# FoX stage of a streaming encoder: turning 128x128 tiles one at a time inside the dense chunk instead of in sets behind it

## The reference

```python
def block(args):
    i, qi, ci = args
    sc = jnp.einsum('bqhd,bkhd->bhqk', qi, k) * SCALE
    sc = sc + ci[..., :, None] - cum[:, :, None, :]
    sc = jnp.where(kpos[None, :] <= qpos[:, None], sc, -jnp.inf)
    p = jax.nn.softmax(sc, axis=-1)
    return jnp.einsum('bhqk,bkhd->bqhd', p, v)
```

## Time and profile before

| | |
|---|---|
| median of 3 runs | 1555.41 us (1554.9 to 1557.6) |
| the profiled execution, span from first to last instruction | 1553.1 us |
| its own time | not among the three runs; its span is the figure for it |
| PE busy (matmul records) | 1495.8 us, 96%, 9803 matmuls |
| DVE, ACT, POOL busy | 1020.4 us (66%), 607.5 us (39%), 611.0 us (39%) |
| chain that ended last | PE 80%, DVE 9% |

### The profile page before, as it was taken

How to read it: one execution, slowest core, us unless ns; L and a number is a source line. 1 busy time by engine, 2 the same in 40 slices (tenths; PEclk the granted TensorE clock), 3 DMA queues, 4 the chain that set the end, 5 groups by cost and what they waited for, 6 DMA issues and landing times.

```text
span 1553.1 us, 25753 instructions
## 1 busy us (share of the span) xinstructions
PE 1495.8 (96%) x9803; PEld 1397.5 (90%) x9803; DVE 1020.4 (66%) x2016; ACT 607.5 (39%) x1256; POOL 611.0 (39%) x407
## 2 busy tenths in 40 slices
PE   6999999999999999999999999999999999999997
PEld 5889999999997998899788999999999999778885
DVE  6866667767674357867445896555555555578986
ACT  5143534435342235666223333333333332444463
POOL 6522232222222322225231568888888781000104
PEclk9999999999999999999999999999999999999999
DMA  6232222222132721129431122222222228723568
GB/s 199 63 94 74 74 87 65 73 70 70 30 97 75 233 95 38 56 82 291 156 108 58 45 67 86 83 83 83 70 83 68 71 83 278 240 97 116 170 195 156
DMA packets 156475, 165.41 MB, mean 107 GB/s; under 512 B 14005, under 2 KB 121913, under 8 KB 156353
## 3 DMA queue, kind: packets, MB, share of 16 engines
q1 hardware_dynamic: 119689, 109.34, 22.6%
q10 hardware_dynamic: 34840, 51.14, 10.0%
q0 software_dynamic: 1824, 3.28, 1.5%
HBM read 125.56 MB, written 39.85 MB: 107 GB/s over the span
## 4 chain that ended last, share of the span: by engine, by line
PE 80%; DVE 9%; DMA 3%; POOL 3%; ACT 2%; issue 2%; ACTq 1%; SPq 0%; DVEq 0%; POOLq 0%
PE bank L1138 16%; PE bank L1140 16%; PE bank L1139 16%; PE bank L1144 6%; PE bank L1146 6%; PE bank L1145 6%; PE bank L1170 4%; PE bank L1279 2%; PE bank L1250 1%; PE bank L1249 1%; DVE p L2649 1%; DVE rowsn L2408 1%; DVE p L2625 1%; POOL ring_l L1080 1%; PE bank L1629 1%
## 5 line engine op out<-in xcount | busy, mean ns | idle before, releaser
L1138 PE MATMUL bank<-ht_h,ring_h 128*128 128x352 f32 x816 | 268.9, 330 | 1.8 <-POOL ring_l L961 1.1
L1140 PE MATMUL bank<-ht_h,ring_l 128*128 128x352 f32 x816 | 263.2, 323 | 0.0
L1139 PE MATMUL bank<-ht_l,ring_h 128*128 128x352 f32 x816 | 262.6, 322 | 0.0
L960 POOL TENSOR_TENSOR ring_h<-raw,att 128x1024 fp32r<-128x1024 f32 x42 | 86.5, 2059 | 405.6 <-PE bank L1140 396.8
L1138 PE MATMUL bank<-m_h,ring_h 128*128 128x264 f32 x648 | 184.2, 284 | 1.2 <-DVE m_l L2895 1.2
L1139 PE MATMUL bank<-m_l,ring_h 128*128 128x264 f32 x648 | 184.2, 284 | 0.0
L1140 PE MATMUL bank<-m_h,ring_l 128*128 128x264 f32 x648 | 183.9, 284 | 0.0
L1138 PEld LDWEIGHTS bank<-ht_h,ring_h 128*128 128x128 f32 x816 | 153.8, 189 | 5.3 <-issue 2.0
L1139 PEld LDWEIGHTS bank<-ht_l,ring_h 128*128 128x128 f32 x816 | 154.6, 189 | 0.7
L1140 PEld LDWEIGHTS bank<-ht_h,ring_l 128*128 128x128 f32 x816 | 153.9, 189 | 0.0
L1138 PE MATMUL bank<-tb_h,ring_h 128*128 128x264 f32 x456 | 129.9, 285 | 0.2 <-DVE u2s L2909 0.2
(11 more groups left out here) (383 smaller groups left out, 3844.9 us busy)
## 6 DMA issues: line engine op xcount, KB each, us to landing
raw<-in_w_up SPq DMA_DIRECT2D x44, 512.0 KB, 3.9
raw<-in_w_in SPq DMA_DIRECT2D x34, 512.0 KB, 3.9
rb<-in_w_down SPq DMA_DIRECT2D x66, 256.0 KB, 2.9
d_y<-conv SPq DMA_DIRECT2D x22, 529.0 KB, 3.3
d_gate<-gst ACTq DMA_DIRECT2D x48, 176.0 KB, 1.9
a<-d_y SPq DMA_DIRECT2D x33, 256.0 KB, 6.1
ra<-d_y SPq DMA_DIRECT2D x33, 256.0 KB, 3.1
gm<-d_gate ACTq DMA_DIRECT2D x8, 528.0 KB, 4.4
```

What stands on the lines that cost most here:

```text
L960: order.link(nc.gpsimd.tensor_tensor(high, src, zero.to_broadcast(list(src.shape)), ALU.add))
L1138: nc.tensor.matmul(out, wh, xh, start=start, stop=False, skip_group_check=onto)
L1139: nc.tensor.matmul(out, wh, xl, start=False, stop=False, skip_group_check=onto)
L1140: return nc.tensor.matmul(out, wl, xh, start=False, stop=stop, skip_group_check=onto)
```

## The change

`dense_chunk` gets a function `turn`, called behind each of its 24 matmuls with the number m of the matmul (0 to 23). In FoX steps with a chunk this function issues the turns one by one, never two behind the same matmul: with n probability tiles, turn j goes behind matmul 24-n+j, so the last one stands behind the chunk's last matmul. In row steps, row tiles 0 to 7 go behind matmuls 0 to 7 and the ninth behind matmul 22-n. The grouping into sets, the banks, the number of turns, and what ACT, DVE and POOL do stay as they are; the waits for a free bank stand before the first turn of each set, that for p_ready before the first probability turn, and that for the keys or values before the first row turn. Without a chunk the turns are issued as before. The row tiles of step (0,0) stay behind the chunk.

```diff
--- before.py
+++ after.py
@@ -1145,7 +1145,11 @@
                 nc.tensor.matmul(out, th, wl, start=False, stop=False, skip_group_check=onto)
                 return nc.tensor.matmul(out, tl, wh, start=False, stop=stop, skip_group_check=onto)
 
-            def dense_chunk(n, c, k_tiles=KT, xh=ht_h, xl=ht_l, col=0, q=None):
+            def no_turn(m):
+
+                return
+
+            def dense_chunk(n, c, k_tiles=KT, xh=ht_h, xl=ht_l, col=0, q=None, turn=no_turn):
 
                 q = position(n, c) if q is None else q
                 pe.wait_ge(slab_split, n + 1)
@@ -1153,11 +1157,16 @@
                 s = n % NSPL
                 wh = flat(ring_h[:, s]).rearrange("p (k c) -> p k c", k=k_tiles)
                 wl = flat(ring_l[:, s]).rearrange("p (k c) -> p k c", k=k_tiles)
+                out, sl = bank[q % 3][:, 0:CH], slice(CH * c, CH * c + CH)
                 for k in range(k_tiles):
-                    mm = three(bank[q % 3][:, 0:CH], wh[:, k, col:col + P], wl[:, k, col:col + P],
-                               xh[:, k, CH * c:CH * c + CH], xl[:, k, CH * c:CH * c + CH],
-                               k == 0, k == k_tiles - 1)
-                mm.then_inc(chunk_full, 1)
+                    nc.tensor.matmul(out, wh[:, k, col:col + P], xh[:, k, sl], start=k == 0, stop=False)
+                    turn(3 * k)
+                    nc.tensor.matmul(out, wh[:, k, col:col + P], xl[:, k, sl], start=False, stop=False)
+                    turn(3 * k + 1)
+                    mm = nc.tensor.matmul(out, wl[:, k, col:col + P], xh[:, k, sl], start=False, stop=k == k_tiles - 1)
+                    if k == k_tiles - 1:
+                        mm.then_inc(chunk_full, 1)
+                    turn(3 * k + 2)
 
             ti = [0]
 
@@ -1254,12 +1263,31 @@
                                               start=False, stop=True)
                     mm.then_inc(s_full, 1)
 
-            def prob_transposes(g):
-                h, b, r = UNITS[g % NU]
-                pe.wait_ge(p_ready, g + 1)
-                assert ti[0] == at_unit[g]
-                for o, w in halves(b, r):
-                    transposes(lambda bk: [(bk[:, i:i + P], ssb[:, g % 2, o + i:o + i + P]) for i in range(0, w, P)])
+            def prob_turn(g, j):
+
+                tiles = width(*UNITS[g % NU][1:]) // P
+                i = at_unit[g] + j // 4
+                if j == 0:
+                    assert ti[0] == i
+                    pe.wait_ge(p_ready, g + 1)
+                if j % 4 == 0:
+                    wait(pe, t_free, i - 1)
+                mm = nc.tensor.transpose(tbank(i)[:, P * (j % 4):P * (j % 4) + P], ssb[:, g % 2, P * j:P * j + P], ident)
+                if j % 4 == 3 or j == tiles - 1:
+                    mm.then_inc(t_full, 1)
+                    ti[0] += 1
+
+            def row_turn(src, i0, j):
+
+                i = i0 + j // 4
+                if j % 4 == 0:
+                    assert ti[0] == i
+                    wait(pe, t_free, i - 1)
+                r = rows(j)
+                mm = nc.tensor.transpose(tbank(i)[0:r, P * (j % 4):P * (j % 4) + P], src[:, P * j:P * j + r], ident)
+                if j in (3, 7, NT):
+                    mm.then_inc(t_full, 1)
+                    ti[0] += 1
 
             def values(v):
                 p, j = divmod(v, V_PAIR)
@@ -1305,22 +1333,33 @@
                         if s % HEAD_U == 0:
                             pe.wait_ge(kq_ready, 2 * p + s // HEAD_U + 1)
                         scores(p, s)
-                    for n, c in fillers(p, s) if g else ():
-                        dense_chunk(n, c)
                     if p == 0 and s == 0:
 
                         pe.wait_ge(freed_dve, reads["dve"][slab_end(SLAB["fv", 0])])
                         row_tiles(vqn)
-                    if s == K_ROWS[p]:
-
-                        pe.wait_ge(freed_dve, reads["dve"][first_chunk[VALUES[p + 1]]])
-                        row_tiles(ktn)
-                    if s == V_ROWS[p]:
-
-                        pe.wait_ge(freed_dve, reads["dve"][first_chunk[QUERIES[p + 1]]])
-                        row_tiles(vqn)
-                    if g >= 1 and s <= NU:
-                        prob_transposes(g - 1)
+                    tiles = width(*UNITS[(g - 1) % NU][1:]) // P if g >= 1 and s <= NU else 0
+
+                    def chunk_turn(m):
+
+                        if m == 0 and s == K_ROWS[p]:
+                            pe.wait_ge(freed_dve, reads["dve"][first_chunk[VALUES[p + 1]]])
+                        if m == 0 and s == V_ROWS[p]:
+                            pe.wait_ge(freed_dve, reads["dve"][first_chunk[QUERIES[p + 1]]])
+                        if s in (K_ROWS[p], V_ROWS[p]):
+                            src, i0 = (ktn, at_row[p + 1][0]) if s == K_ROWS[p] else (vqn, at_row[p + 1][1])
+                            if m < 8:
+                                row_turn(src, i0, m)
+                            if m == 22 - tiles:
+                                row_turn(src, i0, 8)
+                        if 24 - tiles <= m:
+                            prob_turn(g - 1, m - 24 + tiles)
+
+                    chunks = fillers(p, s) if g else []
+                    for n, c in chunks:
+                        dense_chunk(n, c, turn=chunk_turn)
+                    if not chunks:
+                        for j in range(tiles):
+                            prob_turn(g - 1, j)
 
 
             n = SLAB["gate", 10]
```

## The result

| | before | changed |
|---|---|---|
| median of 20 runs each, us | 1555.16 (1551.89 to 1560.16) | 1558.9 (1555.2 to 1563.36) |
| ratio, 95% interval | | 1.0021 (1.0012 to 1.0031) |
| profiled execution: span, own time, us | 1553.1, not among the runs | 1555.7, 1557.53 |

By the interval the change costs 1.9 to 4.8 us; the ratio itself gives 3.3, the difference of the medians 3.7. The time lies in the range (1551 to 1561), 3.0 us above the predicted one, and the ratio lies at the bound of 0.2%, the point estimate just beyond it. So "within 0.2%" was a near miss, on the slow side.

What follows compares the result with a forecast made beforehand. PE was taken to bound the kernel, with 80% of the chain. Terms of +1.5, -1.0 and 0.0 gave +0.5 us; with 2.3 carried over from the profiled span of 1553.1, 1555.9 us, range 1551 to 1561.

Steps and rivals of the forecast that it cites:

- Term 1: All turns moved between dense matmuls: each costs 0.11 us as in a set, perhaps 0.005 more; 292 turns, +1.5 us.
- The first rival: Turns between dense matmuls become nearly free because their weights load under the long matmul in front; 1541 us, chance 4%.
- (0,2): Pair 0, step 2, which already waits for its probabilities: one dense matmul more behind the wait, +0.2 us.
- (0,14): Pair 0, step 14: POOL moves by 0.46 us, its second operation delays DVE's readout and a turn; +0.5 us.
- (p,7): Step 7 of pairs 1 to 3: DVE's small operation gets in before POOL's second operation; -0.11 us each, -0.3 in all.
- Term 2: Eight row steps: two 0.58 us gaps each go, new stalls come because banks are still held; sum -1.0 us.
- (0,7): Pair 0, step 7, a key row step: the first row turn stalls 1.91 us for DVE's readout, so +0.75 us.
- Terms 3 and 4: Probability turns wanted earlier in the chunk, and POOL's phase shifted against DVE; together 0.0 us (-1 to +5).
- (p,13): Step 13 of pairs 1 to 3: the fifth turn's wait for the readout gets 0.14 us shorter, -0.4 in all.
- The second: Rival: in step 7 of pairs 1 to 3 DVE's L2491 misses the gap between POOL's operations; 1560.5 us, chance 19%.
- The third: Rival: in row steps the eviction waits simply go and the first row turn finds its bank free; 1547.6 us, 9%.
- The fourth: Rival: the compiler or the queue puts the turns back in sets, so the sum is 0; chance 1%.

Runs made afterwards that it cites:

- the best version: Against the kernel before: row turns 0-7 behind matmuls 5-12, ninth behind 15, probability turns in sets, DVE's readout ahead of the maximum in row steps; 1544.8 us, ratio 0.9923.
- the kernel with the longer stall: The change, with the first row turn waiting until both banks of the step before are free, instead of one; 1567.3 us, ratio 1.0070 against the kernel before.

## Why the prediction was right or wrong

**What bounds the stage.** Right. PE's stream counts one for one, the idle before turns was for L2408, and it went from the row steps. The prediction counts all 7.8 us to them; 6.6 are theirs, and 1.2 belong to (0,0). The sum doesn't use the 7.8.

**Term 1, the price of a turn.** Right: 0.11 us in a set and between dense matmuls, pairs 0.27 apart. The first rival is refuted. With the probability turns alone, the stage without (0,2), (0,14) and (p,7) is +0.74, where I had 0.005 for each of its 208 turns between dense matmuls, 1.0. The Trainium skill (TensorE: Matmul & The Clock Gate, Back-to-back issue gap) gives some 81 ns for a 128-column pair; the rows here have 0.11 in both placements, and the measurement decides.

**Term 2, row turns.** The mechanism was right in all eight steps: gaps gone, and a new wait for L2315 at the first row turn, or at the fifth in the value steps. The sizes: sum -1.0 predicted, -0.43 measured, or about -0.7 against that if the turns' own price, 84 x 0.0036 = 0.3, is taken out of the measured sum. The part that I had mis-sized is how soon PE goes on. I had put 0.05 us from the end of the readout to the turn. In (0,7) the first readout ends at 121.01 and the turn starts at 121.16, and the other four first row turns also start 0.15 us after it. So the stall of (0,7) is 2.01 (the turn comes 2.22 behind D0, of which 0.21 is its normal place) and not 1.91. The trace of before has both values: 0.05 at the ninth row turn, 0.15 at the first probability turn behind it.

**Terms 3 and 4.** (0,2) right. (0,14) +0.72 for +0.5: POOL's second operation holds DVE for 1.66 us and the first readout ends 3.63 us behind the step's mask matmul, both as forecast, but the turn starts 0.15 us after that end, where I had put nothing. (p,7) right, by a margin of 0.05 us on which I had put a fifth of the chances; which side it fell on was luck.

(p,13) gained 0.17 in all and not 0.42. The mechanism is right, and with the rows alone the size too, -0.16 a step for the forecast -0.14; a term is missing. POOL's L960 takes longer when a DVE operation with two SBUF operands is still running as it starts. Before, and in the best version:

```profile
248.35 1.22 DVE L2429 TENSOR_TENSOR kl<-ktn,kh 64x1024 fp32r<-64x1024 f32 x1
249.03 2.29 POOL L960 TENSOR_TENSOR ring_h<-raw,att 128x1024 fp32r<-128x1024 f32 x1 [16.41 <-PE bank L1140]
```

```profile
244.09 1.22 DVE L2466 TENSOR_TENSOR kl<-ktn,kh 64x1024 fp32r<-64x1024 f32 x1
245.45 1.89 POOL L960 TENSOR_TENSOR ring_h<-raw,att 128x1024 fp32r<-128x1024 f32 x1 [12.97 <-PE bank L1166]
```

L960 starts 4.3 us behind the mask matmul of (1,12) in both, but takes 2.29 us where DVE is still at L2429 for half a microsecond, and 1.89 where DVE is through. L961 follows it, and L961 holds L2491 and with it the readout that the fifth turn waits for. So what counts is how far DVE is through with this operation when POOL starts. With the rows alone at the chunk's start DVE is 0.18 us earlier, L960 takes 2.11 and the step gives -0.16. In the change DVE gains the same 0.19, but the turns inside the chunk of (1,12) start POOL 0.34 later; L961 comes only 0.06 earlier than before, and the step gives -0.06. This shift of POOL, which I had reckoned for the other steps, I left out here. It is also the 0.3 us by which (p,13) makes the whole worse than the sum of its two parts. That the row steps get shorter isn't enough: the late rows shorten them by a microsecond, but there DVE is no earlier (L960 2.31, +0.02).

**The sum, and the step that failed.** The steps together give +0.9 for +0.5. The medians give +3.7. The 0.4 us between forecast and steps are about what the late restarts of PE (0.1 us at each of the five first row turns, 0.15 at (0,14)) and the missing term in (p,13) add up to, less what the key steps give back. The larger miss is a premise of the second term, that a stall costs its length ("stall 1.91, so +0.75"). It failed. A stall of 2.0 us in the chunk is followed, in some executions, by 3.4 us of PE at half clock, and costs 1.55 us more. The trace of before had a place where this could be asked: PE stands for 1.84 us in (0,2), and there the clock stayed up. I took that for granted in the new places. Over the profiles of this study:

| stand of PE (idle in the profile) | profiles or steps with it | clock fell behind it |
|---|---|---|
| (0,2), 1.8 to 2.0 us, in every kernel | 14 profiles | 3 |
| first row turn of (0,7), 1.8 to 2.1 us | 6 profiles | 4 |
| first row turn of (0,9) and the key steps, made longer, 1.9 us | 4 steps | 2 |
| (0,9) and key steps, row turns as in the change, 1.3 to 1.4 us | 5 profiles, 20 steps | 0 |

In the three profiles of the change the stage is +0.9, +2.5 and +4.0, a mean of +2.5. Two of the three falls in them are behind the new stall of (0,7). The third is behind (0,2), where before stands too, for 1.84 us against 2.0 in the change; of the seven profiles with the shorter stand one has a fall there, of the seven with the longer one two. Whether the change has a part in that one isn't shown; without it the mean is +1.9. The Trainium skill (TensorE: Matmul & The Clock Gate, Part 1: The HAM clock gate) says that the gate's watch runs free of the program, so that the same kernel pays differently from run to run. The trace agrees: 0, 1 and 2 falls in the stage in three profiles of one kernel.

**What stays open.** From +2.5 to +3.7, about 1.2 us, is within the interval of the ratio (from +1.9). Two more numbers bear on it. When the change was run again, the difference of the medians was +2.4, and the medians of before in the later batches, 1555.7, 1556.6 and 1556.1, all lie above the 1555.2 of the first; so a part of the +3.7 is most likely scatter of the batch. And each execution, profiled or not, has a mean granted clock: over 32 of the change it is 0.9914 (0.9912 in the first batch, 0.9918 in the second), over 65 of before in three later batches 0.9921. Taken over 1557 us the difference is 1.1 us of clock, and the mean times of the same executions differ by 2.5 us. The 0.9 from the steps and 1.1 from the clock make 2.0, and the 2.5 is uncertain by about 0.5 (the standard error of the two means). The batches weren't run side by side, and these means don't say where in the kernel the clock fell. Behind the stage, between 460 and 1540 us, half clock takes 10.2, 6.8 and 13.6 us in the three profiles of before, and 13.6, 20.4 and 6.8 in those of the change, and three profiles of each can't tell these apart.

**Rivals.** The first is refuted. The second is a real mechanism, shown by forcing it, and did not occur. The third (waits simply go) did not occur in the change, but one swap in DVE's order makes it true, and then it gives -7.95 for the -7.8 that I had worked out. The fourth did not occur: turn and dense matmul alternate.

## What to carry to other kernels

Moving work between the matmuls of a dense chunk gains nothing by itself where its price is the same in both places; it gains what the waits around it cost, and only if its buffer is free at the new place. So first ask who frees the buffer and what stands ahead of that on the freeing engine: here the change as it is loses 0.2%. With the row turns started some matmuls later it gains 0.3%, with the readout moved ahead of the maximum 0.5%; and with the probability turns left in sets, the later row turns alone give 0.6%, both together 0.8%. Price a stall of PE of some 2 us inside dense work above its length. Compare parts of a kernel by the distances of one instruction per step, which here repeat to 0.1 us where medians scatter by several.

## What was unexpected of the hardware

- The granted clock fell to 0.50 behind stands of 1.8 to 2.1 us of PE between dense work, in 9 of 24 cases of the table, never behind 20 of 1.3 to 1.4 us. It came 0.1 to 1.5 us after PE went on, stayed for 3.4 us and cost 1.5 to 1.6 us each time.
- A 128x1 operation on DVE took 0.16 us when it started 0.05 us ahead of a POOL operation, and 2.35 us when it started 0.06 behind it; 3.8 us of kernel time hung on that over three steps.
- PE started a turn 0.05 us after the end of the DVE operation that freed its bank in some places and 0.15 in others (0.10 at the first row turns of the kernel with the longer stall). What decides between them isn't shown.
